# A two-block transformer on one core: in the second block's mixers, key rows copied by transfers, two loads with an earlier wait, and another order of VectorE's list

## What is computed

```python
proj = h @ w_in                                   # c_q 384, c_kv 256, k_pe 32, gate_b, gate_c, val 512 each
q = (rms_norm_2(c_q, q_a_norm) @ w_uq).reshape(B, S, 8, 96)        # 64 plain columns, 32 with rope
kv = (rms_norm_2(c_kv, kv_a_norm) @ w_ukv).reshape(B, S, 8, 128)   # 64 key, 64 value columns
k_pe = apply_rope(k_pe[:, :, None, :], cos, sin)                   # one set of 32, for all 8 heads
k_full = jnp.concatenate([k_nope, jnp.broadcast_to(k_pe, (B, S, N_HEADS, QK_ROPE_DIM))], axis=-1)
attn = causal_attention(q_full, k_full, v)        # 128-query blocks; block i reads keys [0, (i+1)*128)
conv = gate_b * causal_short_conv(gate_c * val, conv_w)
merged = jnp.concatenate([rms_norm_2(attn, attn_out_norm), rms_norm_2(conv, conv_out_norm)], axis=-1)
return merged @ w_o
```

## Time and profile before

| | |
|---|---|
| runs | 3626.56, 3628.98, 3636.25 us |
| median | 3628.98 us |
| the profiled execution's own time | 3625.59 us |
| its span, first to last instruction | 3623.8 us, mean granted TensorE clock 0.997 |
| TensorE busy | 3565.8 us, 98% |
| VectorE, ScalarE, GpSimd busy | 2033.3, 1294.1, 63.6 us |
| first mixer of the second block | about 2040 to 2235 us of the span |
| second mixer | about 3015 to 3210 us |

### The profile page before, as it was taken

How to read it: one execution, slowest core, us unless ns; L and a number is a source line. 1 busy time by engine, 2 the same in 40 slices (tenths; PEclk the granted TensorE clock), 3 DMA queues, 4 the chain that set the end, 5 groups by cost and what they waited for, 6 DMA issues and landing times.

```text
span 3623.8 us, 46522 instructions
## 1 busy us (share of the span) xinstructions
PE 3565.8 (98%) x17492; PEld 2868.1 (79%) x17492; DVE 2033.3 (56%) x3405; ACT 1294.1 (36%) x2112; POOL 63.6 (2%) x112
## 2 busy tenths in 40 slices
PE   9999999999999999999999999999999999999999
PEld 7777777888866788888888777888888887778887
DVE  5777766655766566566333667533453347574334
ACT  4445544322243232233223344322332334443232
POOL 0000000000000000000000000000000000000000
PEclk9999999999999999999999999999999999999999
DMA  4222213655521255652233222233323322123332
GB/s 141 73 74 74 76 62 105 207 176 191 186 64 47 76 201 177 214 192 92 93 98 94 71 68 76 87 99 95 96 91 96 99 93 69 62 73 99 97 95 81
DMA packets 141561, 386.22 MB, mean 107 GB/s; under 512 B 21424, under 2 KB 62768, under 8 KB 141392
## 3 DMA queue, kind: packets, MB, share of 16 engines
q1 hardware_dynamic: 126928, 306.39, 26.7%
q0 software_dynamic: 14464, 77.60, 6.3%
HBM read 381.85 MB, written 2.10 MB: 106 GB/s over the span
## 4 chain that ended last, share of the span: by engine, by line
PE 88%; DVE 7%; issue 3%; ACT 2%; DMA 0%; SPq 0%; DVEq 0%; ACTq 0%
PE psP L1084 25%; PE psP L1089 24%; PE psP L1085 24%; PE psP L1239 3%; PE psP L1246 3%; PE psP L1240 3%; PE psS L1302 1%; PE psS L1582 1%; PE psS L1176 1%; PE psM L1605 1%; PE psS L1468 1%; PE psS L1452 0%; DVE w_lo L2268 0%; DVE w_lo L1698 0%; DVE w_more_lo L1928 0%
## 5 line engine op out<-in xcount | busy, mean ns | idle before, releaser
L1084 PE MATMUL psP<-h_hi,w_hi 128*128 128x512 f32 x2664 | 1053.7, 396 | 4.8 <-ACT h_hi L697 1.8
L1085 PE MATMUL psP<-h_hi,w_lo 128*128 128x512 f32 x2664 | 1038.2, 390 | 0.0
L1089 PE MATMUL psP<-h_lo,w_hi 128*128 128x512 f32 x2664 | 1028.8, 391 | 0.0
L1698 DVE TENSOR_TENSOR w_lo<-raw,w_hi 128x1024 fp32r<-128x1024 f32 (+1 forms) x465 | 557.7, 1199 | 412.1 <-ACT w_hi L654 403.1
L660 ACT ACTIVATE ybuf<-psP 128x512 f32<-128x512 f32 (+1 forms) x401 | 239.3, 597 | 1229.5 <-PE psP L1089 1227.9
L1084 PEld LDWEIGHTS psP<-h_hi,w_hi 128*128 128x128 f32 x2664 | 500.7, 188 | 132.8 <-issue 32.2
L1089 PEld LDWEIGHTS psP<-h_lo,w_hi 128*128 128x128 f32 x2664 | 498.5, 188 | 109.2 <-DVE h_lo L1779 5.1
L1085 PEld LDWEIGHTS psP<-h_hi,w_lo 128*128 128x128 f32 x2664 | 501.1, 188 | 99.2
L654 ACT ACTIVATE w_hi<-raw 128x1024 fp32r<-128x1024 f32 (+1 forms) x465 | 480.7, 1034 | 102.8 <-PE psP L1089 102.8
L1084 PE MATMUL psP<-a_hi,w_hi 128*128 128x512 f32 x1248 | 492.3, 395 | 1.2 <-ACT a_hi L1037 1.2
L1085 PE MATMUL psP<-a_hi,w_lo 128*128 128x512 f32 x1248 | 485.7, 389 | 0.0
(11 more groups left out here) (320 smaller groups left out, 3575.2 us busy)
## 6 DMA issues: line engine op xcount, KB each, us to landing
raw<-in_gu SPq DMA_DIRECT2D x264, 512.0 KB, 3.4
adaw<-in_ada POOLq DMA_DIRECT2D x96, 768.0 KB, 5.1
raw<-in_down SPq DMA_DIRECT2D x96, 448.0 KB, 3.4
raw<-in_down SPq DMA_DIRECT2D x48, 512.0 KB, 3.6
raw<-in_qkv SPq DMA_DIRECT2D x40, 512.0 KB, 3.6
raw<-in_mix_in SPq DMA_DIRECT2D x34, 512.0 KB, 3.5
raw<-in_qkv SPq DMA_DIRECT2D x64, 256.0 KB, 3.0
raw<-in_wo SPq DMA_DIRECT2D x32, 512.0 KB, 3.4
```

The source lines that it names most:

```text
L1084: nc.tensor.matmul(psP[:, s, :], hi, rhs[0](kt), start=(n == 0), stop=False)
L1085: nc.tensor.matmul(psP[:, s, :], lo, rhs[0](kt), start=False, stop=False)
L1089: mm = nc.tensor.matmul(psP[:, s, :], w_hi[:, s, kt * P:kt * P + P], rhs[1](kt), start=False, stop=(n == K - 1))
L1698: v.tensor_tensor(w_lo[:, s, 0:cols], raw[:, s, 0:cols], w_hi[:, s, 0:cols].bitcast(F32), ALU.subtract)\
```

## The change

Four things are changed, all of them in the second block's mixer, so each happens twice.

- GpSimd's two copies of the key rows are replaced by seven transfers of 32 rows of 512 floats (64 KB each) from SBUF to SBUF, issued from GpSimd's queue when head 0's rows are there. They count on a new semaphore, `kpe_spread`; TensorE's scores of head 1 wait for all seven, those of head 0 for VectorE alone.
- The loads of query tiles 1 and 2 wait for the `w_lo` of the last tile that had weights in their own slot, not of the tile three places earlier, which had none.
- ScalarE moves value tiles 2 and 3 out ahead of rounding query tile 1; VectorE takes key tiles 0 and 1 ahead of query tile 1's `w_lo`.
- In the loop, VectorE's `output` of heads 0 to 6 stands ahead of `masked(n + 3)`. A tile that ends in the last two units of its step is finished one step later, behind that step's mask (and, in steps 28 to 31, behind the output parts). `squares_before` stands behind such a late tile.

```diff
-def finished_in(n):
-    return [(kind, k) for kind, k, kt in step_units(n) if kt == kt_of(kind) - 1]
+def finished_in(n, soon=None):
+
+    units = step_units(n)
+    last = [i for i, (kind, k, kt) in enumerate(units) if kt == kt_of(kind) - 1]
+    return [units[i][:2] for i in last if soon is None or soon == (i < len(units) - 2)]
...
-            def load(src, cols=D):
-
-                sp.wait_ge(lo_done, pos.free(0))
+            def load(src, cols=D, weightless=0):
+
+                sp.wait_ge(lo_done, pos.free(-weightless))
...
-                for (kind, k), cols in zip(MIXER[6:], MIXER_COLS[6:]):
+                for i, ((kind, k), cols) in enumerate(zip(MIXER[6:], MIXER_COLS[6:])):
+                    weightless = {K_STEP + 4: 2, K_STEP + 5: 3}.get(i + 6, 0)
                     if kind == "q":
-                        load(one(A["uq"], l * 8 + k), cols)
+                        load(one(A["uq"], l * 8 + k), cols, weightless)
...
-                pool.wait_ge(kpe_ready, 3 * l + 1)
-                pe_rows = k_early[64:96, 0:1, :]
-                nc.gpsimd.tensor_copy(k_early[64:96, 1:4, :], pe_rows.broadcast_to((32, 3, T))).then_inc(kpe_ready, 1)
-                nc.gpsimd.tensor_copy(k_late[64:96, :, :], pe_rows.broadcast_to((32, 4, T))).then_inc(kpe_ready, 1)
+                pool.wait_ge(kpe_ready, l + 1)
+                for h in range(1, 8):
+                    pool.dma_start(k_of(h)[64:96, :], k_early[64:96, 0, :]).then_inc(kpe_spread, 16)
...
-                prep(K_STEP + 4, early=6)
                 values(2)
                 values(3)
+                prep(K_STEP + 4, early=6)
                 prep(K_STEP + 5, early=3)
...
-                        pe.wait_ge(kpe_ready, 3 * l + (1 if h == 0 else 2 if h < 4 else 3))
+                        if h == 0:
+                            pe.wait_ge(kpe_ready, l + 1)
+                        elif h == 1:
+                            pe.wait_ge(kpe_spread, 112 * (l + 1))
...
-                prep(K_STEP + 4)
                 for b in range(4):
                     pos.step()
                 dve.wait_ge(evac_done, pos.count(RING))
                 keys(0)
                 keys(1)
+                prep(K_STEP + 4)
                 masked(0)
...
                 for n in range(32):
                     h, i = divmod(n, 4)
+                    if h < 7 and i == 3:
+                        output(h, slice(0, 4))
                     if n + 3 < 32:
                         masked(n + 3)
-                    if 24 <= n < 28:
-                        squares_before(n - 24)
                     if h == 7:
                         output(h, slice(i, i + 1))
                         squares_after(i)
-                    elif i == 3:
-                        output(h, slice(0, 4))
                     if n >= 29:
                         attn_lo(n - 29)
                     if n >= 28:
                         attn_scaled(n - 28)
-                    finish(finished_in(n))
+                    if n:
+                        finish(finished_in(n - 1, False))
+                    if 24 <= n < 28:
+                        squares_before(n - 24)
+                    finish(finished_in(n, True))
+                finish(finished_in(31, False))
```

More of the change, by code:

```diff
@@ L472, in program @@
         angle_ready, sin_ready, lpar_ready = sem("angle_ready"), sem("sin_ready"), sem("lpar_ready")
-        gain_turned, gain_ready, kpe_ready, key_scale_ready, qscale_ready, q2_ready = (
-            sem(n) for n in ("gain_turned", "gain_ready", "kpe_ready", "key_scale_ready", "qscale_ready", "q2_ready"))
+        gain_turned, gain_ready, kpe_ready, kpe_spread, key_scale_ready, qscale_ready, q2_ready = (
+            sem(n) for n in ("gain_turned", "gain_ready", "kpe_ready", "kpe_spread", "key_scale_ready", "qscale_ready", "q2_ready"))
         scores2, masked2, exp2_done, turned2, probT2_ready, pv2_done, o2_ready = (
@@ L611, in _ @@
                     else:
-                        load(one(A["mix_in"], l * 17 + (5 + 3 * k + ("gate_c", "value", "gate_b").index(kind))))
+                        load(one(A["mix_in"], l * 17 + (5 + 3 * k + ("gate_c", "value", "gate_b").index(kind))), D, weightless)
                 load_many(lambda m: one(A["wo3"], l * KT + m), KT)
```

## The result

The changed kernel took 3606.81 us (median of 4 runs, 3604.73 to 3607.99) against 3629.88 us before (4 runs, 3626.56 to 3636.25): 23.1 us less, ratio 0.9936 with a 95% interval of 0.9921 to 0.9951. The forecast was 3612 us in a range of 3605 to 3620. The profiled execution took 3606.76 us with a span of 3605.0 us, 18.8 us less than the span before. Which of the two it was has to be read from the mechanism.

The account below looks back on a forecast made before the run. TensorE, busy 98% of the span, was taken as the bound, with only its idle stretches to win. Terms of 4.15, 2.71, 0.54, 0.19 and 0.07 us make 7.66 per mixer, 15.3 in two: 3612 us, range 3605 to 3620.

Parts of the forecast that it names:

- Which of the two it was: The forecast proper, 3608 to 3616 us, or the rival that the loop gives nothing back, 3606 to 3609 us, chance 0.14.
- the rival in whose band the median lies: Loop gives nothing back: all 5.3 us of `o_tok` waits go, 4.5 in the prologue; 3606 to 3609 us, chance 0.14.
- Prologue, 4.15 us: Before the loop: VectorE's unbroken run from masked scores 0 to query 1, not TensorE's idle, sets 4.15 us per mixer.
- Transfers at nothing: Seven key-row transfers at 3.0 us land by about 2080.6, before head 1's scores at 2089.9; cost nothing, cover 7 to 9.
- Head 4, 2.71 us: Step 16: with mask 17 ahead of value 1, `output` is ready early and the whole 2.71 us wait goes.
- Head 2, 0.54 us: Step 8: only mask 10 and the output swap, bringing the output 0.54 us forward; 0.76 us of the wait stays.
- Heads 6 and 7, 0.19 us: Steps 24 to 28: the 0.90 us wait goes but returns at step 26; about 0.19 of 1.26 us remains won.
- Steps 28 to 31, 0.07 us: Output transposes: a `w_lo` moves behind step 29's output part; 0.5 us of wait goes, 0.45 returns, 0.07 won.
- Sum, 15.3 us: All prologue and loop terms: 7.66 us per mixer, 15.3 us in two mixers.

Follow-up runs that it names:

- the two parts alone: Kernel before with only the seven transfers: 3625.33 us, ratio 0.9986; kernel before with only the earlier loads and swapped prologue order: 3623.66 us, ratio 0.9983.
- experiment 9: Changed kernel with each of the seven transfers issued only when the one before has landed: 3611.59 us, ratio 0.9949 to the kernel before.
- experiment 5: Changed kernel with no tile finished late, the output still ahead of the mask: 3616.63 us, ratio 0.9962 to the kernel before.
- experiment 7: Changed kernel with query 3 finished late too: 3607.26 us, ratio 0.9939 to the kernel before.
- experiments 1, 2 and 3: Kernel before with the transfers alone (3625.33 us), the loads and prologue order alone (3623.66 us), and both together (3619.34 us).
- experiments 4 to 12: Loop alone on the kernel before (3615.59 us), then the changed kernel with late tiles, `w_lo`, query 3, transfers or copies altered, or repeated; ratios 0.9930 to 0.9962.
- experiments 11 and 12: Changed kernel run again: 3609.68 us; changed kernel with query 3 late and two `w_lo` behind step 24's mask, run again: 3605.26 us.

## Why the prediction was right, point by point

By its mechanism the forecast came true and the rival in whose band the median lies did not: 0.8 us of the `o_tok` waits is left, and 1.27 us is given back between steps 25 and 26. That the time still fell into that rival's band is partly the clock, which neither of them had priced.

- **Prologue, 4.15 us.** Measured 4.34 and 4.19, with the two parts alone at 2.8 and 1.9 to 2.0. Both mechanisms are shown, and so is it that the two parts do not add up in full. That VectorE's run decides is read from the trace: TensorE waits 0.56 us for query 1 before head 1's scores, where it was 0.34. These scores come 4.35 us earlier after the key rows; after the spread, as I had worded it, only 2.9 us earlier, since the spread itself has moved.
- **Transfers at nothing.** Right, with 1.8 to 1.9 us each in place of my 3.0. With the seven overlapping, the last lands at 2076.0, 13.7 us ahead of head 1's scores, so the cover was larger than the 7 to 9 us forecast; without the overlap it is used up (experiment 9).
- **Head 4, 2.71 us.** Measured 2.86 (7.84 - 4.98 in the first mixer); experiment 5 ties it to the late tiles.
- **Head 2, 0.54 us.** Measured 0.54 (4.98 - 4.44 at step 4), and 0.76 left, of which experiment 7 takes all.
- **Heads 6 and 7, 0.19 us.** Measured 0.26 (8.19 - 7.93, step 28 against steps 17 to 22): the give-back happened two steps later, as forecast. One part was read wrong: I had the whole of it on `probT` (1.0 us), but 0.62 of it is TensorE's wait for query 7, one step sooner, and 0.26 `probT`. I had followed VectorE to the mask and not asked who needs the query in between.
- **Steps 28 to 31, 0.07 us.** Mis-sized: at the third transpose of the output rows the kernel is 8.68 us ahead, 0.49 more than at step 28. The wait that goes, before the second transpose, is worth 0.68 us with the slow restart behind it. The wait before the first, which I had at 0.6 as before, is 0.72. The wait that I expected before the third (0.45) is about 0.2, since the transpose starts 1.05 us behind step 31's `weigh` (2205.54 - 2204.49) where it was 0.84 before (2214.17 - 2213.33).
- **Sum, 15.3 us.** In both profiles' first mixers the first matmul of the output projection (2232.22 and 2223.64) comes 8.63 us earlier; twice this is 17.3. Of the 2 us that the sum lacks, 0.7 is the term of steps 28 to 31 (0.44 us per mixer up to the output projection, 0.07 forecast); the rest is 0.1 to 0.2 us per mixer in the prologue, at head 4 and in the steps between. What the sum left out is the clock: I took the durations of the matmuls as given behind a wait. The fall of the clock after the 2.7 us wait was in the trace of before, 1.6 us in the second mixer, and I had looked at the first mixer's timeline alone and at a mean clock of 0.997. The profiled executions differ by 17.3 + 1.6 = 18.9 us, which is the 18.8 of their spans. The medians differ by 23.1. The 4 us more are within the interval (its bounds are 18 and 29 us), and they are likely the clock's as well: the mean granted clock was 0.995 on average over the 40 runs of before beside the experiments, 0.997 over the four of the changed kernel, and the profiled execution of before, at 0.997, was among its least disturbed. Of those 40 runs the four at 0.997 have spans of 3624.4 us on average, the seven at 0.993 of 3629.5. Where in these runs the clock fell is not known.

## What to carry to other kernels

When TensorE's named waits are short, replay each engine's list in order with the trace's durations: the gain is what is left after the work put off meets the next deadline, here 8.6 us of 10 in the waits per mixer. Where two kernels lie closer than their runs, compare stretches from a mark that no edit touches: here the steps repeat within 0.03 us from one profile of the changed kernel to the next, its runs only within 8 us. A helper on GpSimd should be placed by what VectorE reads at that moment rather than replaced at once. And a wait of a few us on TensorE is dearer than its length if the granted clock falls behind it; look at the clock in stretches after each of the longest waits, not at its mean.

## What the runs showed of the hardware that was not expected

- Of eight mixers with the 2.7 us wait before step 16 (the kernel before and experiments 1, 2 and 3), five had the granted clock at its lower level behind it, for 3.4 us and 1.6 us of lost time: all four second mixers, but only one of the four first ones; of 20 without that wait (experiments 4 to 12 and the changed kernel, 0 to 2.2 us in its place) none had it at step 16. Two of the 20 had a wait of 2.15 us there. The lists do not settle which mixers fall, and no run changed the length of that wait alone, so that the wait is the cause is likely but not shown.
- The same happened around the end of the 2.0 us wait of experiment 9 (0.76 and 0.82 in 2088 to 2096 us, 0.64 in 3060 to 3064). The clock fell ahead of the first mixer as well (experiments 11 and 12); what stood before those falls was not followed up.
- The Trainium skill (TensorE: Matmul & The Clock Gate, Part 1) lists two states of the clock gate, half and full, 1.2 and 2.4 GHz. The trace agrees: matmuls of 512 columns took 0.63 us at the low level and 0.39 at the full one, and clocks between the two appear only as means over a stretch.
- 64 KB from SBUF to SBUF took 1.8 to 1.9 us with seven in flight, and 2.15 to 4.3 us from one issue to the next when each waited for the last. With loads of weights in flight such a transfer took 2.5 to 4.0 us, without 1.9 (experiment 9).
